# Hybrid attention and gated-delta layer: order of requests, filler and read-back in the delta scan

## The reference, cut to what matters

```python
h = rms_norm(x, norm1_g) * (1.0 + sc1) + sh1
aq, ak, av, dq, dk_, dv_, dz, dbeta, dalpha, ga, gb = jnp.split(h @ w_in, split_idx, axis=-1)
# delta rule, per chunk: T is the inverse of (I + strictly lower part of (k_beta k^T) * decay)
lmat = jnp.where(tril_strict, einsum('id,jd->ij', k_beta, k) * decay, 0.0)
t_inv = triangular_solve(eye + lmat, eye)
u, w = t_inv @ v_beta, t_inv @ (k_beta * exp(g))
def step(state, xs):                      # 256 context tokens, then 1024 latent ones
    v_new = u_i - w_i @ state
    o_i = (q_i * exp(g_i)) @ state + a_i @ v_new
    state = state * exp(g_last) + (k_i * exp(g_last - g_i)).T @ v_new
merged = sigmoid(ga) * (o_a @ w_pa) + sigmoid(gb) * (o_d @ w_pb)
x = x + g1 * (merged @ w_o)
x = x + g2 * ((silu(h2 @ w_gate) * (h2 @ w_up)) @ w_down)
```

## Time and profile before

| | |
|---|---|
| median of 3 runs | 2965.82 us (2961.95 to 2968.04) |
| the profiled execution | 2968.09 us, its span 2966.3 us |
| busy PE, DVE, ACT, POOL over the span | 2681.6, 1400.3, 1040.5, 606.5 us |
| mean granted TensorE clock | 0.942 of full |

### The profile page before, as it was taken

How to read it: one execution, slowest core, us unless ns; L and a number is a source line. 1 busy time by engine, 2 the same in 40 slices (tenths; PEclk the granted TensorE clock), 3 DMA queues, 4 the chain that set the end, 5 groups by cost and what they waited for, 6 DMA issues and landing times. The chain is left out here.

```text
span 2966.3 us, 46114 instructions
## 1 busy us (share of the span) xinstructions
PE 2681.6 (90%) x18134; PEld 2525.5 (85%) x18134; DVE 1400.3 (47%) x2320; ACT 1040.5 (35%) x1801; POOL 606.5 (20%) x489
## 2 busy tenths in 40 slices
PE   7999999589898999828999869989999999999999
PEld 3898999578888888726777758889999999999999
DVE  3565331157666766447888833352222242222222
ACT  4312332233343333136778733322222222222211
POOL 1001222434333433143323221210111000111100
PEclk9999999779897999858999979999999999999999
DMA  5324664334343433140000044332222233222232
GB/s 202 144 80 131 220 220 153 101 91 111 100 151 80 122 85 86 59 163 14 9 17 16 12 181 166 116 99 71 78 78 71 78 114 94 71 78 72 69 96 70
DMA packets 194779, 294.22 MB, mean 99 GB/s; under 512 B 82704, under 2 KB 121648, under 8 KB 192816
## 3 DMA queue, kind: packets, MB, share of 16 engines
q1 hardware_dynamic: 191728, 276.15, 29.6%
q10 hardware_dynamic: 2880, 15.73, 1.5%
HBM read 228.28 MB, written 63.52 MB: 98 GB/s over the span
## 5 line engine op out<-in xcount | busy, mean ns | idle before, releaser
L277 PE MATMUL f_ps<-mf_h_hi,mf_w_hi 128*128 128x320 f32 x1408 | 435.1, 309 | 1.4 <-PEq L1982 1.4
L277 PE MATMUL f_ps<-mf_h_hi,mf_w_lo 128*128 128x320 f32 x1408 | 435.1, 309 | 0.0
L277 PE MATMUL f_ps<-mf_h_lo,mf_w_hi 128*128 128x320 f32 x1408 | 435.1, 309 | 0.0
L2415 DVE TENSOR_TENSOR mf_w_lo<-mf_w_raw,mf_w_hi 128x1024 fp32r<-128x1024 f32 (+1 forms) x135 | 188.8, 1399 | 431.6 <-ACT mf_w_hi L2267 431.4
L277 PE MATMUL proj_ps<-h_hi,w_hi 128*128 128x320 f32 x896 | 282.7, 316 | 6.0 <-DVE w_lo L575 5.6
L277 PE MATMUL proj_ps<-h_hi,w_lo 128*128 128x320 f32 x896 | 278.0, 310 | 0.0
L277 PE MATMUL proj_ps<-h_lo,w_hi 128*128 128x320 f32 x896 | 278.0, 310 | 0.0
L277 PEld LDWEIGHTS f_ps<-mf_h_hi,mf_w_hi 128*128 128x128 f32 x1408 | 264.4, 188 | 1.6 <-issue 1.6
L277 PEld LDWEIGHTS f_ps<-mf_h_lo,mf_w_hi 128*128 128x128 f32 x1408 | 264.4, 188 | 0.0
L277 PEld LDWEIGHTS f_ps<-mf_h_hi,mf_w_lo 128*128 128x128 f32 x1408 | 264.4, 188 | 0.0
L2341 POOL TENSOR_TENSOR f_ff_lo<-f_ff_f,f_ff_hi 128x640 f32 (+1 forms) x44 | 69.3, 1576 | 783.1 <-ACT f_ff_hi L2267 783.1
(11 more groups left out here) (323 smaller groups left out, 6425.2 us busy)
## 6 DMA issues: line engine op xcount, KB each, us to landing
mf_w_raw<-w_up_dram SPq DMA_DIRECT2D x88, 512.0 KB, 3.5
w_ada_raw<-w_ada_dram SPq DMA_DIRECT2D x16, 1024.0 KB, 5.2
mf_w_raw<-w_mix_dram SPq DMA_DIRECT2D x32, 512.0 KB, 5.0
w_raw<-w_in_dram SPq DMA_DIRECT2D x28, 512.0 KB, 5.1
mf_w_raw<-w_down_dram SPq DMA_DIRECT2D x32, 448.0 KB, 3.3
delta_t<-delta_tile ACTq DMA_DIRECT2D x10, 1024.0 KB, 6.7
fill_raw<-w_in_dram SPq DMA_DIRECT2D x20, 512.0 KB, 4.2
kq_t<-delta_t SPq DMA_DIRECT2D x20, 512.0 KB, 4.3
```

Source lines behind the costliest of these rows:

```text
L277: ins = nc.tensor.matmul(out, w(k), a(k), start=(first and n == 0 and q == 0), stop=(last and n == len(ks) - 1 and q == 2))
L2415: nc.vector.tensor_tensor(wlo[:, slot, 0:nk], raw[:, slot, 0:nk], whi[:, slot, 0:nk].bitcast(F32), ALU.subtract).then_inc(E[half]["lo"], 1)
```

## The change

Five edits, all about the scan:

1. The first requests of the scan are now rows 0, keys 0, the two masks, rows 1, keys 1, keys 2, then the initial state. In the profile before they were masks, two weight tiles, the initial state, and only then keys and rows. The zeroing of `XB` goes from POOL to DVE, and SP waits for it only at its first use.
2. The fill weights use the projection's own buffers (`w_raw`, `w_hi`, `w_lo`), which live on through the scan; the projection's last two steps load fill tiles 0 and 1 and split tile 0. To make room, `ada_and_norm` places its small arrays inside others, and SP asks for the first two weight tiles only after the 16 transposes of the modulation rows (`cols_done`).
3. Filler starts in unit -2 with two matmuls a slot (26 in that unit), goes on with four from unit -1, rests in unit 8 instead of unit 9, and so ends a unit earlier on either side.
4. The read-back of `h_late`, two requests of 2.5 MB in slot 2 of unit 8, becomes 16 requests of 320 KB in four groups: at the end of unit 7 and at three places of unit 8.
5. The context state is stored in unit 6 instead of unit 4.

```diff
@@ ada_and_norm, SP
             sp.dma_start(bg_raw[:], io["w_bg"]).then_inc(bg_in, 16)
+            sp.wait_ge(cols_done, 1)
             for p in range(2):
                 sp.dma_start(keep["w_raw"][:, p], io["w_in"][p]).then_inc(keep["w_in_sems"][p], 16)
@@ in_projection, SP, ACT, DVE: the tile after the last is loaded and split too
-                if t + 2 < FILL0:
-                    sp.wait_ge(lo_ready, t + 1)
-                    sp.dma_start(raw[:, t % 2], io["w_in"][t + 2]).then_inc(w_in[t % 2], 16)
+                sp.wait_ge(lo_ready, t + 1)
+                sp.dma_start(raw[:, t % 2], io["w_in"][t + 2]).then_inc(w_in[t % 2], 16)
...
-                if t < LAST:
-                    split_hi(t + 1, (t + 1) % 2, (t + 1) // 2 + 1)
+                split_hi(t + 1, (t + 1) % 2, (t + 1) // 2 + 1)
...
-                if t < LAST:
-                    split_lo(t + 1, (t + 1) % 2)
+                split_lo(t + 1, (t + 1) % 2)
@@ delta_scan, plan of the filler
+        RELOAD = 8
+        def quota(u):
+            return {-3: 0, -2: 2, RELOAD: 0}.get(u, 4)
         for u in UNITS:
             for s in range(SLOTS):
-                plan(u, s, 4 if -1 <= u < NT - 1 or u >= NT else 0)
...
+                t, i = divmod(at[0], PER)
+                n = min(quota(u), 3 * KT - i % (3 * KT))
+                pieces[u, s] = []
+                if n and t < (FILL_TILES if u < RELOAD else NF):
+                    pieces[u, s] = [(t, i // (3 * KT), i % (3 * KT), i % (3 * KT) + n)]
+                    at[0] += n
@@ delta_scan, SP
+            def reload(u, i):
+                n = 4 * (u - RELOAD) + i + 1
+                if 0 <= n < 4:
+                    if n == 0:
+                        sp.wait_ge(e["fill_ps"], 2 * FILL_TILES)
+                    for k in (2 * n, 2 * n + 1):
+                        for part, h in enumerate((h_hi, h_lo)):
+                            sp.dma_start(h[:, k].bitcast(F32), io["h_late"][part][:, k]).then_inc(e["h2_in"], 16)
...
-                        if t == FILL_TILES - 1:
-                            sp.dma_start(h_hi[:].bitcast(F32), io["h_late"][0]).then_inc(e["h2_in"], 16)
-                            sp.dma_start(h_lo[:].bitcast(F32), io["h_late"][1]).then_inc(e["h2_in"], 16)
+            load_rows(0)
+            load_kq(0)
             for name in ("offdiag", "levels"):
                 sp.dma_start(keep[name][:], io[name]).then_inc(e["masks_in"], 16)
-            load_weights(0)
-            load_weights(1)
+            load_rows(1)
+            load_kq(1)
+            load_kq(2)
...
-            sp.wait_ge(e["xb_zero"], 1)
             for u in UNITS:
-                if has(u + 3):
-                    if u < 0:
-                        load_kq(u + 3)
+                if has(u + 3) and u >= -1:
                     load_rows(u + 3)
+                reload(u, 0)
...
-                if u == 4:
+                reload(u, 1)
+                if u == 6:
                     sp.wait_ge(e["s_ready"], 4)
...
                 if has(u + 2):
                     blocks_out(u + 2)
+                reload(u, 2)
...
                 if has(u + 2):
                     blocks_in(u + 2)
+                reload(u, 3)
@@ delta_scan, POOL, then DVE
-            nc.gpsimd.tensor_scalar(XB[:].rearrange("p t h i -> p (t h) i"), keep["ident"][:].unsqueeze(1).to_broadcast([P, 2 * NH, P]), 0.0, None, ALU.mult).then_inc(e["xb_zero"], 1)
...
+            nc.vector.tensor_scalar(XB[:].rearrange("p t h i -> p (t h) i"), keep["ident"][:].unsqueeze(1).to_broadcast([P, 2 * NH, P]), 0.0, None, ALU.mult).then_inc(e["xb_zero"], 1)
```

More of the change, by code:

```diff
@@ L68, in ada_and_norm @@
         c_raw = sb("c_raw", [P, KT, 2])
-        rows = sb("mod_rows", [2, ADA1 * P])
-        bg_raw = sb("bg_raw", [P, KT, 32])
-        bg_hi = sb("bg_hi", [P, KT, 32], F32R)
-        bg_lo = sb("bg_lo", [P, KT, 32], F32R)
-        bg_t = sb("bg_rows", [32, T])
+        rows = keep["w_raw"][0:2].rearrange("p t k n -> p (t k n)")
         hf = sb("h_f32", [P, HR, 3 * P])
+        bg_raw = hf[:, HR - 1, 0:KT * 32].rearrange("p (k n) -> p k n", k=KT)
+        bg_hi, bg_lo = (keep["w_lo"][:, p, 0:2].rearrange("p k n -> p (k n)").rearrange("p (k n) -> p k n", k=KT) for p in range(2))
+        bg_t = lambda b: x[0:32, TAPS[b][0], 0:span(b)[1] - span(b)[0]]
         sq = hf[:].rearrange("p r n -> p (r n)")[:, 0:D]
@@ L225, in _ @@
                 for j in range(*TAPS[b]):
-                    last = nc.tensor.transpose(col_ps[:, 32 * j:32 * j + 32], bg_t[:, j * P:(j + 1) * P], keep["ident"][0:32, 0:32])
+                    last = nc.tensor.transpose(col_ps[:, 32 * j:32 * j + 32], bg_t(b)[:, (j - TAPS[b][0]) * P:(j - TAPS[b][0] + 1) * P], keep["ident"][0:32, 0:32])
             last.then_inc(bg_cols, 1)
@@ L286, in in_projection @@
         ROWS, DR0 = NT * NH, CONV_TILES + 1
-        raw = keep["w_raw"]
-        whi = sb("w_hi", [P, 2, KT, P], F32R)
-        wlo = sb("w_lo", [P, 2, KT, P], F32R)
+        raw, whi, wlo = keep["w_raw"], keep["w_hi"], keep["w_lo"]
         padded = sb("conv_in", [P, 2, PADDED])
@@ L781, in delta_scan @@
         ost = sb("o_stage", [P, 2, 512])
-        fraw = sb("fill_raw", [P, 2, KT, P])
-        fhi = sb("fill_hi", [P, 2, KT, P], F32R)
-        flo = sb("fill_lo", [P, 2, KT, P], F32R)
+        fraw, fhi, flo = keep["w_raw"], keep["w_hi"], keep["w_lo"]
         fout = sb("fill_stage", [P, 2, 2, GN])
@@ L799, in delta_scan @@
         o_stored = [sem(f"o_stored{i}") for i in range(2)]
-        fw_in = [sem(f"fill_in{i}") for i in range(2)]
+        fw_in = keep["w_in_sems"]
         f_stored = [sem(f"fill_stored{i}") for i in range(2)]
@@ L1081, in body @@
                     fill(u, s)
-            split_hi(0)
             for u in UNITS:
@@ L2553, in build @@
         }
+        keep["w_in_sems"] = [ctx.enter_context(nc.semaphore(f"w_in{p}")) for p in range(2)]
         keep["first_sem"] = ctx.enter_context(nc.semaphore("first_sem"))
@@ L2559, in build @@
             h_lo = [c0.enter_context(nc.sbuf_tensor("h_lo0", [P, KT, HT], F32R))]
+            keep["w_raw"] = c0.enter_context(nc.sbuf_tensor("w_raw", [P, 2, KT, P], F32))
+            keep["w_hi"] = c0.enter_context(nc.sbuf_tensor("w_hi", [P, 2, KT, P], F32R))
+            keep["w_lo"] = c0.enter_context(nc.sbuf_tensor("w_lo", [P, 2, KT, P], F32R))
             with ExitStack() as c1:
@@ L2563, in build @@
                 keep["c_act"] = c1.enter_context(nc.sbuf_tensor("c_silu", [P, KT, 2], F32))
-                keep["w_raw"] = c1.enter_context(nc.sbuf_tensor("w_raw", [P, 2, KT, P], F32))
-                keep["w_in_sems"] = [c1.enter_context(nc.semaphore(f"w_in{p}")) for p in range(2)]
                 keep["b_ada"] = c1.enter_context(nc.sbuf_tensor("b_ada_sb", [P, 48], F32))
```

40 lines of the change are left out of this document (16 added, 24 removed).

## The result

The changed kernel takes 2944.44 us (median of 6 runs, 2937.4 to 2953.99) beside 2965.98 (6 runs, 2961.95 to 2972.29): ratio 0.9925, 95% interval 0.9909 to 0.994. The forecast was 2945.4, 20.4 less than before; the medians lie 21.5 apart. The profiled run took 2941.67 us, its span is 2939.9 us, 26.4 less than before. Medians of different series can't be compared directly, since the kernel before moved from 2961.28 to 2967.24 between them; the ratios can. This kernel scatters over 17 and 24 us where the one before, beside it in the same two series, scattered over 10 and 12; part of what follows is about why.

A forecast was written before the change was run, and what follows sets the result against it. It took each unit to be bound nearly equally by PE's work and a 29.55 us ring through SP. Opening -10.6, state -8.8, read-back -3, tail +2 sum to -20.4 us: 2945.4 against the median 2965.8, range 2932 to 2958.

The forecast's parts named there:

- The opening: Scan's start to unit 0's first product: rows and keys requested sooner, one split out of the way; -10.6 us.
- the split's 1.2 us: DVE's fill split in the middle of the first inversion would come behind it, saving 1.2 us.
- rows requested 9.0 earlier: Unit 0's rows asked for at 554.03 instead of 563.03; with faster landing, 9.4 us on the chain.
- rival D: Opening: the scan's chain starts on something else, as masks for POOL; -10.6 falls to about -1, 2955 us; chance 0.08.
- ring: Each unit's chain through SP, one `diag_inv` to the next, 29.55 us; binds at nearly the same length as PE's work.
- rival B: Opening filler keeps PE's clock up; about 6 us more gain, -26 in all, 2939 us; chance 0.15.
- The state: Store moved from unit 4 to 6: 11.4 us of excess vanish, 2.6 of issue are added; net -8.8 us.
- upper bound of -5: State store in unit 6: the issue paid twice over, as its small transfers also delay the next; only -5 us.
- The read-back: Units around the `h_late` read-back: 11.8 us excess becomes 8.7 (groups 6.0, following stretch without filler 2.7); -3 us.
- Rival A: Read-back pieces lie on the critical chain: +10 instead of -3, -7.4 in all, 2958 us; chance 0.12.
- The projection and filler at nothing: Projection's added loads and split, and filler in unit -2, are covered by other work or waits: 0 us.
- Tail: Units 18 and 19 without filler: one weight store less, but slower clock; +2 us net, bounds -1 and +9.

The follow-up runs named there:

- `b_first`: The kernel before with only the changed order of the scan's first requests; 2964.72 us, ratio 0.999.
- `a_dry`: The changed kernel without filler in unit -2, its 26 matmuls given to unit 3; 2952.14 us, ratio 0.9967.
- `b_state`: The kernel before with the context state stored in unit 6 instead of unit 4; 2960.02 us, ratio 0.9973.
- `a_slack`: The changed kernel with state store and all four read-back groups moved behind the `diag_blocks` requests (ends of units 6 and 7); 2941.43 us, ratio 0.9918.
- `a_best`: The changed kernel, store behind `diag_blocks` in unit 6, groups 1-2 there in unit 7, 3-4 in unit 8, a semaphore per group; 2934.68 us, ratio 0.9904.
- `a_sem`: The changed kernel with a semaphore per read-back group, waited for at the matmul first reading it; 2948.09 us, ratio 0.9941.
- second profile: The changed kernel, unchanged, timed and profiled again in a later series; 2949.54 us, ratio 0.9948.
- `a_whole`: As `a_slack`, but the read-back as two requests of 2.5 MB instead of sixteen of 320 KB; 2944.95 us, ratio 0.9922.

## Why the prediction was right, and where it wasn't

**The opening, -10.6: right in size, -11.5, wrong in one reason.** Rows landed 4.0 us after the request (4.7 taken, 4.0 was the bound), and the inversion lost the split's 1.2 us as named (1.1 measured). Two terms that were not named cancel: the stretch from the first `diag` request to the one for `diag_blocks` took 4.8 us instead of 6.0, and the factors took 1.0 longer between ACT and DVE, since POOL first waits for the second mask, now landing after the rows, and then runs one product in 2.24 us instead of 1.27.

```profile
560.26 2.50 POOL L1022 TENSOR_TENSOR decay_t<-decay_t,tri_sb 128x512 f32<-128x512 f32 x2 [3.52 <-DMA levels_sb<-levels_dram]
```

That wait costs 0.5 us and is rival D's mechanism in small. The wrong reason: the step "rows requested 9.0 earlier" was credited to the order of requests, with the projection edits at nothing. `b_first` shows the order alone at no gain; it needs the first fill tile split elsewhere. The error was to follow SP's list and not ACT's: the first instruction of ACT's list before was a split that waited for weights.

**Rings 0 to 4, not forecast, -2.1.** Two rings are 6.4 us shorter (61.8 to 55.4) and ring 3 is 2.9 longer. From 620 to 640 the clock is at 0.90 instead of 0.50. That is rival B's effect in size; its cause, the filler, explains a part at most by `a_dry`, and the same code gave 58.9 in another profile. What ends the low clock sooner stays open.

**The state, forecast -8.8: right mechanism, mis-sized.** Rings 5 to 7 gained 5.1, about the upper bound of -5 (the reason given for that bound, the issue paid twice over, would make -6.2). The long ring fell by 10.5 (11.4 forecast); the store in its new place cost about 5 (35.1 against 30.2 for its neighbour), not its 2.58 us of issue. In `b_state` the two terms came as forecast, -8.1 together, and `a_slack` and `a_best` have the store at no cost, 30.6 and 30.7. Laid beside the same ring of `a_best`, the 4.4 us of difference are 2.6 of issue, 1.1 by which the key and `diag` requests behind the store took longer (4.62 against 3.75 us for `diag`), 0.2 in `diag_inv`'s landing, and 0.4 behind `diag_blocks`.

**The read-back, forecast -3: the sum right by luck.** Rings 8 to 11: -5.1 in one profile, +6.5 in the other, -2.7 in `a_sem` (130.5). Groups 1 and 2 were nearly free, as said (30.2; 28.6 in `a_best`, where they stand behind `diag_blocks`). Ring 9 with groups 3 and 4 took 37.2, 7 over its neighbours, where 6.0 was forecast for the groups; but `a_best` has 35.1 there with no group ahead of `diag_blocks`. So some 2 us are the groups' and 5 the missing filler's. The prediction had that loss in the following ring, at 2.7, as in the kernel before, and overlooked that unit 8 now has both; the following ring took 30.2. The two errors nearly cancel (67.4 us measured for the two rings, 67.8 by its working). The wait of PE's filler in unit 9 for the last piece was not priced at all; only the ring was looked at. Rival A, pieces on the ring, was thus a little true, by another wait than the one it named.

**The projection and filler at nothing.** What stands behind the scan moved by 0.6 us. Within the opening edit 2 takes away the wait without which the order gained nothing, see above.

**Tail, forecast +2: +3.4**, 5.3 in the second profile. Its length goes with the clock, as the bound of +9 had in mind: from 20 to 30 us behind the last `diag_inv` it was at 0.50 in both profiles of the kernel after (tails of 57.2 and 59.1), at 0.83 before (53.8), and at 1.00 in `a_slack` and `a_whole`, with the code of the kernel after (47.8 and 48.4). So even the sign of what the change does to the tail isn't shown.

**Rings 12 to 18, -5.0, not forecast**, -2.8 in the second profile. Nothing in them was changed but which filler they hold. Eight profiles with this code took 209.9 to 217.5 us, four of the kernel before and those built on it 212.7 to 217.4: chance, as far as the record goes.

The terms' errors don't cancel within a profile. Against the forecast the first profile has state +3.7, opening -0.9, read-back -2.1, rings 0 to 4 -2.1, rings 12 to 18 -5.0, tail +1.4, the rest -1.0: -6. The second has read-back +9.5, state +2.9, tail +3.3, rings 12 to 18 -2.8 and the others -1.6: +11. The median of the first series lies between them, and that it came within 1.1 us of the forecast (-21.5 against -20.4) is luck beyond what the single terms deserve; the second series' ratio is some 15 us of gain.

## What to carry to other kernels

When a request is moved ahead, read the head of every list that consumes it, not only of the one that issues it: one instruction that waits for something now asked for later eats the whole gain. On a queue that is on a critical ring, put the bulk where its issuer waits anyway, and no more of it than lands before the next small transfer; its size per request mattered less here than its place. A ring passes through the lists of all engines in it: where a copy that the ring waits for stands behind one that waits for filler, late filler lengthens the ring. A semaphore for each part, waited for by the first reader of that part, cost nothing measurable here, and alone it gained nothing measurable either. And where one kernel scatters by 24 us, a term read from a single profile needs a second one.

## What the runs showed of the hardware that was not expected

- TensorE at its low level while it was busy throughout: 20.00 of 20 us from 620 to 640 at 0.50 before. The Trainium skill (TensorE: Matmul & The Clock Gate, Part 1) has activity raise the clock; this row does not agree. `a_dry`, with more idle time ahead than the kernel after, had the same 0.90 from 620 to 640, but 19 us of low clock from 600 to 660 instead of 12 and 14.
- A small transfer behind bulk waits for the bytes: 128 KB of `diag_inv` had its successor start after 2.3 us with nothing ahead, 2.6 behind 2.6 MB asked for 7 us or more earlier, 9.0 right behind 5.2 MB in pieces, 7.1 behind 5.2 MB whole whose requests ended 12.5 us earlier.
- Two profiles of one kernel differed by 8.3 us in a single ring, and by at most 0.1 in each of the first five; another kernel with the same code up to there (`a_slack`) differed by 3.3 in the first.
- The zeroing of 128x2048 took 5.36 us on POOL (kernel before, 557.25) and 1.23 on DVE (kernel after, 552.39).
